# Queries from the un-normed first-residual stream, with the cross attention's scores, heads and output projection interleaved

## The reference, cut to what matters

```python
def layer_norm(x, g, b):
    mu = x.mean(-1, keepdims=True)
    var = jnp.square(x - mu).mean(-1, keepdims=True)
    return (x - mu) * lax.rsqrt(var + EPS) * g + b

def memory_cross_attention(x, mem, wq, wkv, wo):     # 4 heads of 256
    q = (x @ wq).reshape(B, S, 4, 256)
    k, v = jnp.split(mem @ wkv, 2, axis=-1)
    ...
    p = jax.nn.softmax(einsum('bshd,bmhd->bhsm', q, k) * 256 ** -0.5, axis=-1)
    return einsum('bhsm,bmhd->bshd', p, v).reshape(B, S, 1024) @ wo

h = hybrid_mixer(x, ...)                             # ends in @ w_out
x = layer_norm(ALPHA * x + h, ln1_g, ln1_b)
h = memory_cross_attention(x, mem, wq, wkv, wo)
x = layer_norm(ALPHA * x + h, ln2_g, ln2_b)
h = conv_ffn(x, ...)                                 # ffn_w_up, ffn_w_down
x = layer_norm(ALPHA * x + h, ln3_g, ln3_b)
```

## Time and profile before

| what | us |
|---|---|
| median of 3 runs | 881.32 |
| the 3 runs | 880.45, 881.32, 883.76 |
| the profiled execution | 883.5 |
| its span, first to last instruction | 881.7 |
| outside the span | 1.8 |
| the last `wout` matmul ends | 182.1 |
| the first query matmul starts | 189.7 |
| the attention's first matmul starts | 215.1 |
| the first `xo` matmul starts | 233.9 |
| the last `xo` matmul ends | 256.7 |
| the first up-projection matmul starts | 264.0 |

### The profile page before, as it was taken

The page is one execution under the profiler, slowest core; times in us unless marked ns, Lnnn a source line. Parts: engine busy times, 40 slices in busy tenths (PEclk is TensorE's granted clock), DMA queues, the critical chain, the costliest instruction groups (busy, mean ns, idle before and its releaser), DMA issues.

```text
span 881.7 us, 15934 instructions
## 1 busy us (share of the span) xinstructions
PE 854.1 (97%) x6420; PEld 808.3 (92%) x6420; DVE 663.2 (75%) x1059; ACT 481.4 (55%) x716; POOL 7.6 (1%) x17
## 2 busy tenths in 40 slices
PE   8999999999999999999997999999999999999997
PEld 7889987989889999999996999898999999999885
DVE  5787797777567888887867896787797687776553
ACT  5643456554547666655456646465557454444452
POOL 0200000000000000000000000000000000000000
PEclk9999999979988999999999999999999999999999
DMA  9887658837152765567762455475565377775761
GB/s 336 243 261 216 205 181 254 248 108 249 31 161 87 226 187 180 182 200 250 263 222 71 142 160 167 135 240 181 169 207 180 96 240 231 225 228 179 153 226 48
DMA packets 139594, 166.91 MB, mean 189 GB/s; under 512 B 5521, under 2 KB 123281, under 8 KB 139521
## 3 DMA queue, kind: packets, MB, share of 16 engines
q1 hardware_dynamic: 137712, 162.82, 59.7%
q0 software_dynamic: 720, 2.02, 1.2%
q10 hardware_dynamic: 1088, 1.05, 0.3%
HBM read 164.62 MB, written 1.25 MB: 188 GB/s over the span
## 4 chain that ended last, share of the span: by engine, by line
PE 72%; DVE 16%; ACT 7%; issue 3%; DMA 1%; SPq 1%; DVEq 0%; ACTq 0%
PE ps L524 71%; DVE lor L1632 6%; DVE FA L1635 3%; DVE FA L1632 2%; ACT hir L1126 2%; DMA raw<-in_w_in 1%; DVE raw L1649 1%; DVE FA L1638 1%; ACT FA L1319 0%; DVE FA L2315 0%; DVE X L1635 0%; ACT FA L1252 0%; ACT FA L1512 0%; PE ps L769 0%; ACT L1141 0%
## 5 line engine op out<-in xcount | busy, mean ns | idle before, releaser
L1632 DVE TENSOR_TENSOR lor<-raw,hir 128x1024 fp32r<-128x1024 f32 (+1 forms) x267 | 309.4, 1178 | 88.3 <-ACT hir L1126 85.5
L1126 ACT ACTIVATE hir<-raw 128x1024 fp32r<-128x1024 f32 (+1 forms) x257 | 258.9, 1031 | 106.0 <-PE ps L524 92.0
L524 PE MATMUL ps<-INH,hir 128*128 128x256 f32 (+2 forms) x1064 | 307.3, 289 | 3.1 <-ACT INH L1294 2.5
L524 PE MATMUL ps<-INH,lor 128*128 128x256 f32 (+2 forms) x1064 | 302.9, 285 | 3.0 <-DVE lor L1632 3.0
L524 PE MATMUL ps<-INL,hir 128*128 128x256 f32 (+2 forms) x1064 | 302.8, 285 | 0.2
L524 PEld LDWEIGHTS ps<-INH,hir 128*128 128x128 f32 x1064 | 204.5, 192 | 5.9 <-issue 4.3
L524 PEld LDWEIGHTS ps<-INH,lor 128*128 128x128 f32 x1064 | 204.4, 192 | 5.4 <-DVE lor L1632 4.3
L524 PEld LDWEIGHTS ps<-INL,hir 128*128 128x128 f32 x1064 | 204.1, 192 | 0.7 <-DVE INL L1632 0.7
L524 PE MATMUL ps<-HIH,hir 128*128 128x256 f32 x688 | 197.4, 287 | 0.0
L524 PE MATMUL ps<-HIH,lor 128*128 128x256 f32 x688 | 194.5, 283 | 0.8 <-DVE lor L1632 0.8
L524 PE MATMUL ps<-HIL,hir 128*128 128x256 f32 x688 | 193.6, 281 | 0.0
(11 more groups left out here) (273 smaller groups left out, 792.1 us busy)
## 6 DMA issues: line engine op xcount, KB each, us to landing
raw<-in_w_in SPq DMA_DIRECT2D x64, 512.0 KB, 4.7
raw<-in_mod_wT SPq DMA_DIRECT2D x48, 512.0 KB, 4.4
raw<-in_ffn_w_up SPq DMA_DIRECT2D x44, 512.0 KB, 4.4
raw<-in_w_ffn_in SPq DMA_DIRECT2D x44, 512.0 KB, 4.7
raw<-in_w_ffn_out SPq DMA_DIRECT2D x22, 512.0 KB, 4.9
raw<-in_ffn_w_down SPq DMA_DIRECT2D x20, 512.0 KB, 4.7
raw<-in_xa_wkv SPq DMA_DIRECT2D x16, 512.0 KB, 4.6
raw<-in_xa_wq SPq DMA_DIRECT2D x8, 512.0 KB, 5.1
```

Of the source, the lines that this page charges most:

```text
L524: return e.matmul(o, l, r, start=start, stop=stop, skip_group_check=True)
L1126: e.activation(hi, src, ACT.Copy).then_inc(*w_hi.up(i))
L1632: return e.tensor_tensor(o, a, b, op)
```

## The change

- Weight order: the three modulation blocks that stood behind the query units move to the down projection (units 0 to 2 take 3 instead of 2). The first halves of `xo` units 0, 1, 2 come before their second halves.
- Behind each `wout` unit, ACT writes the high half of gain times the un-normed residual (`gained`), DVE the low half, into buffer `xg1`, with two extra columns for gain and bias.
- The queries are made by `late_g` from `xg1` (258 columns). The row sums of the norm stand between its first steps, the spreads behind the third; ACT copies the mean and deviation rows to SBUF.
- Each query unit is settled on DVE (per half a small copy and one fused operation, then one multiplication) and ACT (scale -1 and bias). `settle(0)` and `settle(1)` stand ahead of nearly all further splits on DVE.
- Scores 0 and 1 stand between query units 2 and 3; the first halves of `xo` 0 and 1 behind scores 3, that of `xo` 2 behind the last head.
- The norm of X itself (`normed` on DVE, `affine` on ACT), which only the next residual needs, is done between the heads.
- The load of the square root's table stands ahead of the third square instead of behind it.

```diff
-    add2(("xq", 0), A["xa_wq"], 0, ("xq", 1), A["xa_wq"], 256, mod=1)
+    add2(("xq", 0), A["xa_wq"], 0, ("xq", 1), A["xa_wq"], 256)
...
+    for k0 in (0, HALF):
+        for c in range(3):
+            plan.append(((("xo", c), k0), plain(A["xa_wo"], 256 * c, k0, HALF), HALF, True))
+    add(("xo", 3), A["xa_wo"], 768, 8)
...
-        add(("down", c), A["ffn_w_down"], 256 * c, 22, mod=2 + c // 3, spread=True)
+        add(("down", c), A["ffn_w_down"], 256 * c, 22, mod=3, spread=True)
```

TensorE:

```diff
-            layer_norm("n1")
-            run(units_g([("xq", 0), ("xq", 1)], 8, x1))
-            unit(("xq", 2), 8, x1)
-            unit(("xq", 3), 8, x1)
...
+            g = late_g([("xq", 0), ("xq", 1)], xg1, 2)
+            steps_of(g, 1)
+            row_sums("n1", 3, X[:, 6:8, :], g)
+            steps_of(g, 1)
+            spread_bank(("n1", "mu"), SN[:, 0:2])
+            spread_bank(("n1", "r"), SN[:, 6:8])
+            run(g)
...
+            run(late_g([("xq", 2)], xg1, 2))
...
+            scores(0)
+            scores(1)
+            run(late_g([("xq", 3)], xg1, 2))
...
+            turned(0)
+            turned(1)
+            scores(2)
+            head(0)
+            head(1)
+            scores(3)
+            xo = [units_g([("xo", c)], 8, oc) for c in range(3)]
+            next(xo[0])
+            next(xo[1])
+            turned(2)
+            turned(3)
+            head(2)
+            head(3)
+            next(xo[2])
+            for g in xo:
+                run(g)
+            unit(("xo", 3), 8, oc)
```

ACT:

```diff
+            def gained(c):
+                for k in (2 * c, 2 * c + 1):
+                    w.wait_ge(dve.at(("n1", "x", c)), vec_in.at(0), mm.at("xg1 free"))
+                    e.activation(xg1.hi[:, k, 0:T], X[:, k, :], ACT.Copy, scale=V("ln1_g", k)).then_inc(*act.up(("xg1", "hi", k)))
...
+            settle(0)
+            settle(1)
...
             ahead.unit(("xq", 2), 8)
+            expo(0)
+            expo(1)
+            settle(2)
             ahead.unit(("xq", 3), 8)
+            turned(0)
+            turned(1)
+            settle(3)
+            xo = [ahead.units_g([("xo", c)], 8) for c in range(3)]
+            next(xo[0])
+            expo(2)
+            oc_put(0)
+            oc_put(1)
+            expo(3)
+            affine(0)
+            affine(1)
+            next(xo[1])
+            turned(2)
+            turned(3)
+            affine(2)
+            oc_put(2)
+            oc_put(3)
+            next(xo[2])
+            affine(3)
             for c in range(4):
-                ahead.unit(("xo", c), 8)
+                run(xo[c] if c < 3 else ahead.units_g([("xo", 3)], 8))
                 square("n2", c, X[:, 2 * c:2 * c + 2, :], dve.at(("n2", "x", c)), squares_free("n2", "n1", c))
```

DVE (the chain from the sums to the deviation stands ahead of this as before):

```diff
+            def normed(c):
+                d = X[:, 2 * c:2 * c + 2, :]
+                w.wait_ge(act.at("mean row"), act.at(("xg1", "hi", 2 * c + 1)), dve.at(("xg1", "lo", 2 * c + 1)))
+                tt(d, d, over(MB, 2), SUB).then_inc(*dve.up())
+                w.wait_ge(act.at("deviation row"), dve.last())
+                tt(d, d, over(RB, 2), MUL).then_inc(*dve.up(("n1", "normed", c)))
...
+            run(late)
+            settle(0)
+            settle(1)
+            ahead.more()
+            ahead.more()
+            ahead.unit(("xq", 2), 8)
+            settle(2)
+            greatest(0)
+            greatest(1)
+            shares(0)
+            shares(1)
+            ahead.unit(("xq", 3), 8)
+            settle(3)
+            xo = [ahead.units_g([("xo", c)], 8) for c in range(3)]
+            next(xo[0])
+            greatest(2)
+            oc_copy(0)
+            shares(2)
+            oc_put(0)
+            oc_copy(1)
+            greatest(3)
+            oc_put(1)
+            shares(3)
+            normed(0)
+            normed(1)
+            next(xo[1])
+            normed(2)
+            oc_copy(2)
+            oc_put(2)
+            oc_copy(3)
+            oc_put(3)
+            next(xo[2])
+            normed(3)
             for c in range(4):
-                ahead.unit(("xo", c), 8)
+                run(xo[c] if c < 3 else ahead.units_g([("xo", 3)], 8))
                 resid("n2", "xo", c)
                 stats("n2", c, ("n1", "early"))
```

More of the change, by code:

```diff
@@ L1302, in scalar, with settle @@
+            def settle(c):
+                for j in range(2):
+                    w.wait_ge(dve.at((("xq", c), "normed")))
+                    e.activation(QC[:, 2 * c + j, :], QC[:, 2 * c + j, :], ACT.Identity, scale=-1.0, bias=GB2[c % 2][j][:, 1:2]).then_inc(
+                        *act.up(("QC", c)))
             for c in range(4):
                 ahead.unit(("wout", c), 8)
-                square("n1", c, X[:, 2 * c:2 * c + 2, :], dve.at(("n1", "x", c)), squares_free("n1", None, c))
                 if c == 2:
@@ L1306, in scalar @@
                     preload(ACT.Sqrt)
-            layer_norm("n1", "ln1_g", "ln1_b", x1, "x1 free")
+                square("n1", c, X[:, 2 * c:2 * c + 2, :], dve.at(("n1", "x", c)), squares_free("n1", None, c))
+                gained(c)
             act.mark("before cross attention")
-            ahead.units([("xq", 0), ("xq", 1)], 8)
+            late = ahead.units_g([("xq", 0), ("xq", 1)], 8)
+            next(late)
+            w.wait_ge(dve.at(("n1", "var")))
+            e.activation(SN[:, 4:6], SN[:, 2:4], ACT.Sqrt).then_inc(*act.up(("n1", "deviation")))
@@ new lines, in scalar, with affine @@
+            w.wait_ge(mm.at(("n1", "mu")), mm.at(("n1", "early")))
+            e.activation(MB, bank["n1", "mu"][:, 0:T], ACT.Copy).then_inc(*act.up("mean row", ("out", ("n1", "mu"))))
+            run(late)
+            w.wait_ge(mm.at(("n1", "r")))
+            e.activation(RB, bank["n1", "r"][:, 0:T], ACT.Copy).then_inc(*act.up("deviation row", ("out", ("n1", "r"))))
+            ahead.more()
+            ahead.more()
+            settle(0)
+            settle(1)
+            def affine(c):
+                for k in (2 * c, 2 * c + 1):
+                    w.wait_ge(dve.at(("n1", "normed", c)))
+                    e.activation(X[:, k, :], X[:, k, :], ACT.Identity, scale=V("ln1_g", k), bias=V("ln1_b", k)).then_inc(
+                        *act.up(("n1", "affine")))
@@ new lines, in expo @@
+            def expo(i):
+                nmx, rsx = (SX[:, 32 * i + 2 * k:32 * i + 2 * k + 2] for k in (1, 2))
+                for n in range(2):
+                    w.wait_ge(dve.at(("nmx", i)), *([mm.at(("px", i - 2))] if i >= 2 else []), mm.at("before cross attention"),
+                              dve.at("before cross attention"), act.at("before cross attention"))
+                    e.activation(PX[:, i % 2, n, :], bank["lx", i][:, n * T:(n + 1) * T], ACT.Exp, scale=0.0625,
+                                 bias=nmx[:, n:n + 1], accum_out=rsx[:, n:n + 1]).then_inc(*act.up(("out", ("lx", i))))
@@ new lines, in vector @@
+            late = ahead.units_g([("xq", 0), ("xq", 1)], 8)
+            w.wait_ge(mm.at(("n1", "sums")))
+            e.tensor_copy(SN[:, 0:4], bank["n1", "sums"][:, 0:4]).then_inc(*dve.up(("out", ("n1", "sums")), (("n1", "mu"), "factor")))
+            then("mean")
+            tt(SN[:, 8:10], SN[:, 0:2], SN[:, 0:2], MUL).then_inc(*dve.up())
+            then("mean squared")
+            stt(SN[:, 2:4], SN[:, 2:4], LN_EPS, SN[:, 8:10], ADD, SUB).then_inc(*dve.up())
+            then("variance")
@@ new lines, in settle @@
+            def settle(c):
+                key, dst = ("xq", c), QC[:, 2 * c:2 * c + 2, :]
+                for j in range(2):
+                    b, vs = bank["unit", key, j], GB2[c % 2][j]
+                    w.wait_ge(mm.at(("unit", key, j)), *([act.at(("QC", c - 2))] if c >= 2 else []))
+                    e.tensor_copy(vs, b[:, T:T + 2]).then_inc(*dve.up())
+                    w.wait_ge(dve.last(), act.at("mean row"), *before)
+                    stt(dst[:, j, :], MB, vs[:, 0:1], b[:, 0:T], MUL, SUB).then_inc(*dve.up(("out", ("unit", key, j))))
+                w.wait_ge(dve.last(), act.at("deviation row"))
+                tt(dst, dst, over(RB, 2), MUL).then_inc(*dve.up((key, "normed")))
@@ new lines, in greatest, with shares @@
+            def greatest(i):
+                mxx, nmx, rsx = (SX[:, 32 * i + 2 * k:32 * i + 2 * k + 2] for k in range(3))
+                w.wait_ge(mm.at(("lx", i)))
+                e.tensor_reduce(mxx, wide2(bank["lx", i]), AX, MAX).then_inc(*dve.up())
+                then("mxx")
+                ts(nmx, mxx, -0.0625, None, MUL).then_inc(*dve.up(("nmx", i)))
+            def shares(i):
+                rsx = SX[:, 32 * i + 4:32 * i + 6]
+                w.wait_ge(act.at(("out", ("lx", i))))
+                e.reciprocal(rsx, rsx).then_inc(*dve.up())
+                then("rsx")
+                for n in range(2):
+                    ts(PX[:, i % 2, n, :], PX[:, i % 2, n, :], rsx[:, n:n + 1], None, MUL).then_inc(*dve.up(("PX", i)))
```

160 lines of the change are left out of this document (76 added, 84 removed).

## The result

The changed kernel took 886.1 us in the median of 20 runs (883.2 to 888.7), the kernel before 881.8 beside it (880.5 to 886.3): ratio 1.0033, 95% interval 1.0022 to 1.0044, so 2.9 us slower (1.9 to 3.9), where 1.0 us faster was forecast. The profiled execution took 888.07 us, 886.3 of them the span; that is 2.0 over the median of its kernel, as the 883.5 of before are 1.7 over 881.8. One execution of e2, 928.5 us at a mean granted clock of 0.838 in place of 0.98, is left out of its ratio.

A forecast was written before the change was run, and what follows sets the result against it. ACT and DVE handing over in turn, not PE, set the attention's end: last residual 1.8 us earlier, norm tail 7.3 against 6.51, moved blocks nothing. Gain 1.0: 882.5 profiled, 880.3 on the median; range 875.0 to 884.2.

The forecast's parts named there:

- The chain: Attention up to the second norm: ACT and DVE hand-overs in turn put the last residual at 255.7 us, 1.8 earlier.
- PE's `xo`: Attention's output projection: PE's last matmul there ends at 250.6 us, waits included, 6.1 ahead of before's 256.7.
- the waits of PE ahead of the early sums and of X's: Second norm: PE waits some 2.5 us ahead of the early sums and again ahead of X's.
- The first rival: Attention: PE stays the bound as ACT and DVE hand-overs overlap better; 6.1 us gained, 875.2 us; chance 0.22.
- the second: Attention: about 21 changes between ACT and DVE cost 0.2 each, 3.6 us more, 883.9 us; chance 0.14.
- The term of the norm's tail: Second norm: from the last residual to the first up matmul 7.3 us, against 6.51 before.
- the low clock: Second norm: clock low through all the sums, adding 0.8 us for both groups; one group priced at 1.77 against 0.9.
- Moved and small edits: Down projection and small edits: three moved modulation blocks cost 0 to 3.7 us, taken as nothing; wider matmuls 0.2, already counted.
- 34 GB/s more: Down projection, units 0 to 2: the moved modulation loads raise memory traffic by some 34 GB/s over 279.
- the high end of the range: Whole kernel: 884.2 us, the upper end of 875.0 to 884.2, which takes in the second rival.
- the longer chain: Attention: the second rival's case, hand-overs between ACT and DVE at 0.2 each, 3.6 us more; chance 0.14.
- the 6.1 that the forecast gave PE alone: Attention: PE's own work in the new order ends 6.1 us earlier, which becomes a wait before the second norm.

The follow-up runs named there:

- e2: The kernel before with only the three modulation blocks moved into the down projection; 884.6 us, ratio 1.0018 to the kernel before.
- e6: The changed kernel without the norm's own passes on X between the heads (output differs); 880.2 us, ratio 0.9963 to the kernel before.
- e1: The changed kernel with its three modulation blocks put back behind the query loads; 884.9 us, ratio 1.0021 to the kernel before.
- e11: e8 plus matmuls on constants only where PE was seen to wait (9 before X's sums, 6 behind the second spread); 879.7 us, ratio 0.9955 to the kernel before.
- e8: The changed kernel with X's norm passes moved from between the heads to between the first queries' halves, blocks in the up stage; 880.6 us, ratio 0.9969.
- e10: e8 plus 33 matmuls on constants in the second norm's pauses, 12 of them ahead of the early sums; 881.9 us, ratio 0.9987 to the kernel before.

## Why the prediction was wrong

**The chain was right.** The forecast claimed that ACT and DVE in turn, and not PE, set the end. Against W it had the last residual at 73.6 us; it was at 74.2. Block by block on DVE: from `greatest(2)` to the first norm pass 6.6 us (219.30 to 225.91; forecast 6.7), to residual 0 18.2 (to 244.07; forecast 18.0, of which its running sum took 17.7), to the last residual 13.5 (to 257.52; forecast 13.2 and 0.3); `greatest(2)` itself came 0.2 later. PE's `xo` ended at 251.8, or 250.6 on the forecast's scale, as forecast; the waits of PE ahead of the early sums and of X's were there, 2.7 and 1.7 us where some 2.5 each were forecast. The first rival (PE as the bound) is refuted by e6, the second (0.2 for each change of hands) by the blocks. The chain's error is 0.6 us.

**The term of the norm's tail was too small.** It was put at 7.3 us and took 8.05. The eight sums of X and the eight of the squares took 1.73 and 2.10 us; before, where PE had not paused ahead of the early sums, 0.91 and 1.37. The forecast had priced the low clock at 0.8 for both groups; it was 1.55. Its own price of 1.77 for a group would have given 1.3 for both, so the 0.8 doesn't follow from it; and 1.77 is from a row in which the clock fell part-way (granted 0.61 there, 0.50 in both groups of the changed kernel). Together with the chain this makes +0.4 us from W to U where -1.0 was forecast.

**The step that failed is "Moved and small edits".** The blocks were bounded at 0 to 3.7 us and taken at nothing, "since a block stands between splits that have three chunks in hand". e2 and e1 give 1.74, the largest single error of the sum. The busy share was that of the first down unit: 13.29 of DVE in 16, a slack that is real there and hides its blocks in the changed kernel too. From the first unit's end on, a residual and 4.5 us of norm work stand in DVE's queue with a block right behind them. The forecast weighed a block as an operation between splits; what that alone costs is 0.32 us, so there its value of nothing was nearly right. The loads it weighed by their bytes, 34 GB/s more, and not by their order. SyncE waits for a buffer that a late block frees, the DMA moves next to nothing for 2 us, a weight chunk comes 1.42 us late a few chunks further on, and the three chunks in hand don't cover that and the norm's work together: 1.42 us. The bound itself held; the value taken was the wrong end of it.

**The sum.** -1.0 + 0.6 + 0.8 + 1.7 = +2.1 us, against 2.9 measured (1.9 to 3.9). The rest is within the interval, and of the size by which stretches without an edit move (0.6 from U to G, 1.2 up to W, 1.5 from D to H). The forecast of 880.3 stood on a median of 881.32; beside the changed kernel the kernel before had 881.8. Without the blocks the change would still have gained nothing: W to U alone is 0.4 longer. Why a clock that is granted at 1.00 in one execution is 0.79 in the next, in the same stretch with PE full, stays open; no run here told it apart. The measured 886.1 lies 1.9 over the high end of the range: 884.2 had the longer chain in it but not the blocks and the tail beside a chain that was right.

## What to carry to other kernels

Price a moved operation in the stretch of the target stage where its engine is fullest, with the queue just ahead of it, and not by the stage's mean; and where it frees a buffer that loads wait for, follow the load as well. Here three blocks in a row cost 1.74 us, 1.42 of them through one late load; with the same work further apart it was 0.3, and in the up projection nothing. When a wait of TensorE is filled, look at once for the chain that is late next; work that may go anywhere (here the norm's own passes) belongs ahead of that chain, where DVE and ACT are the early ones, which made W to U 4.0 us shorter than in the kernel before, of the 6.1 that the forecast gave PE alone. And compare kernels by stretches between points that PE passes in all of them: here a stretch came back to 0.01 us while whole runs of one program differed by 5.

## What the runs showed of the hardware

The granted clock fell in a stretch in which PE had no idle time at all: 8.01 us for what took 6.49 (0.79 against 1.00), in half of the traces; the stretch begins with some 2.1 us of one-column sums, and the matmuls behind them then start 0.21 us apart in place of 0.12 for part of it. It fell behind waits of 1.28 and 0.37 us in e11 (0.78 over the 7.9 us) and not behind the same waits in e8. Matmuls on constants in the norm's pauses did hold the clock up for the up projection's start (U to G 80.8 in place of 82.6), but each one more than the pause holds delays the chain by its 0.2 us: 12 of them held the early sums up by 2.7 us in e10. A load that waits for a buffer can leave the DMA idle: 53 and 8 GB/s from 416 to 418 us in the changed kernel, against 381 and 386 from 412 to 414.
